# A hybrid decoder step on one core: the head in another order on five engines, past keys and values turned one bank at a time, pooled low halves set between gated products

## The reference, cut to what matters

```python
def compress_kv(kv, w_cmp):               # past rows of the samples: 2048 each
    ch = kv.reshape(B, n_ch, CMP_STRIDE, 2, KV_HEADS, HEAD_DIM)      # CMP_STRIDE = 16
    kc = (einsum('bnjchd,jchd->bnchd', ch[:, :-1], w_cmp[:CMP_STRIDE])
          + einsum('bnjchd,jchd->bnchd', ch[:, 1:], w_cmp[CMP_STRIDE:]))

h = einsum('btd,de->bte', x, w_in)        # layer 0, 3352 columns: values, gates, q, k/v
u = a_val * sigmoid(a_glu)                # then conv, layer norm, attention, w_out

v, gate = split(einsum('btd,de->bte', x, w_in), 2, axis=-1)          # layer 1
d = mean_of_window(v) - v                 # windows 2, 4, 8, 16 on four channel groups
mixed = einsum('btgc,gce->btge', d, w_grp) * scale
y = einsum('bte,ed->btd', mixed * silu(gate), w_out)
```

## Time and profile before

| | |
|---|---|
| median of three runs | 1197.67 us |
| profiled execution, device time | 1204.59 us |
| its span | 1202.9 us |
| PE busy | 1138.5 us (95%) |
| DVE / ACT / POOL busy | 734.9 / 394.8 / 330.4 us |
| chain that ended last, PE's share | 83% |
| DMA moved | 103.17 MB |

### The profile page before, as it was taken

How to read it: one execution, slowest core, us unless ns; L and a number is a source line. 1 busy time by engine, 2 the same in 40 slices (tenths; PEclk the granted TensorE clock), 3 DMA queues, 4 the chain that set the end, 5 groups by cost and what they waited for, 6 DMA issues and landing times.

```text
span 1202.9 us, 17825 instructions
## 1 busy us (share of the span) xinstructions
PE 1138.5 (95%) x7124; PEld 934.8 (78%) x7124; DVE 734.9 (61%) x1360; ACT 394.8 (33%) x838; POOL 330.4 (27%) x340
## 2 busy tenths in 40 slices
PE   5888999999999998999999999899999999989997
PEld 4877999999988854465565655688799999988884
DVE  3467889999883579646544455465555650247645
ACT  3111112122223556565756556411021211244000
POOL 3444530000003577444433434310002212306000
PEclk9899999999999979999999999899999999999999
DMA  6545321353210130004040310832131110131321
GB/s 216 176 158 174 124 89 35 71 196 109 50 40 1 46 140 2 1 1 176 1 176 1 120 57 1 247 120 88 57 92 53 35 52 22 37 140 70 114 96 44
DMA packets 78011, 103.17 MB, mean 86 GB/s; under 512 B 21248, under 2 KB 64392, under 8 KB 76831
## 3 DMA queue, kind: packets, MB, share of 16 engines
q1 hardware_dynamic: 69839, 67.52, 18.2%
q0 software_dynamic: 6016, 33.56, 7.4%
q10 hardware_dynamic: 2080, 1.05, 0.3%
HBM read 90.42 MB, written 16.64 MB: 89 GB/s over the span
## 4 chain that ended last, share of the span: by engine, by line
PE 83%; DVE 8%; DMA 4%; ACT 3%; POOL 1%; issue 1%; SPq 0%; ACTq 0%; POOLq 0%; DVEq 0%
PE PS L681 25%; PE PS L1629 17%; PE PS L1791 14%; PE PS L1165 5%; PE PS L1056 5%; PE PS L1179 4%; PE PS L673 3%; DMA RING<-in_cache_kv_sel,idx 2%; PE PS L1140 2%; PE PS L1094 2%; DVE ACC L548 2%; PE PS L1099 2%; DVE PS L1252 1%; PE PS L1771 1%; DMA idx<-in_page_table 1%
## 5 line engine op out<-in xcount | busy, mean ns | idle before, releaser
L681 PE MATMUL PS<-XH,WH 128*128 128x352 f32 (+1 forms) x648 | 149.2, 335 | 3.1 <-DVE XL L523 3.1
L595 DVE SCALAR_TENSOR_TENSOR Y<-U,SM,Y 128x1024 f32<-128x1024 f32 x120 | 147.4, 1293 | 0.3
L681 PE MATMUL PS<-XL,WH 128*128 128x352 f32 (+1 forms) x648 | 143.7, 326 | 0.0
L681 PE MATMUL PS<-XH,WL 128*128 128x352 f32 (+1 forms) x648 | 143.7, 326 | 0.0
L681 PEld LDWEIGHTS PS<-XH,WH 128*128 128x128 f32 (+1 forms) x648 | 109.0, 188 | 6.5 <-DVE XL L523 3.8
L681 PEld LDWEIGHTS PS<-XL,WH 128*128 128x128 f32 (+1 forms) x648 | 110.5, 188 | 1.4
L681 PEld LDWEIGHTS PS<-XH,WL 128*128 128x128 f32 (+1 forms) x648 | 110.4, 187 | 1.4
L548 DVE SCALAR_TENSOR_TENSOR ACC<-PS,SM,ACC 128x508 f32<-128x508 f32 x124 | 84.0, 740 | 30.7 <-PE PS L673 30.7
L1898 POOL TENSOR_TENSOR WL<-WRAW,WH 128x1024 fp32r<-128x1024 f32 x14 | 37.4, 2673 | 219.8 <-ACT WH L1843 219.8
L1629 PE MATMUL PS<-WOH,XH 128*128 128x512 f32 (+1 forms) x288 | 92.3, 402 | 3.6 <-POOL WOL L1597 3.1
L290 POOL TENSOR_TENSOR WL<-WRAW,WH 128x1024 fp32r<-128x1024 f32 x12 | 28.6, 2385 | 243.2 <-ACT WH L362 235.6
(11 more groups left out here) (316 smaller groups left out, 2057.5 us busy)
## 6 DMA issues: line engine op xcount, KB each, us to landing
WRAW<-in_w_in_even SPq DMA_DIRECT2D x16, 512.0 KB
WRAW<-in_w_in_odd SPq DMA_DIRECT2D x16, 512.0 KB, 4.0
XIN<-in_x_prompt SPq DMA_DIRECT2D x8, 512.0 KB, 12.7
WRAW<-in_w_in_even SPq DMA_DIRECT2D x16, 256.0 KB
TM<-in_state_win_kv SPq DMA_DIRECT2D x8, 512.0 KB, 4.7
XR<-in_x_prompt SPq DMA_DIRECT2D x8, 512.0 KB, 3.5
layer_out<-R SPq DMA_DIRECT2D x8, 512.0 KB, 2.6
XR<-layer_out SPq DMA_DIRECT2D x8, 512.0 KB, 3.2
```

The lines of the kernel that those rows point to most:

```text
L595: v.scalar_tensor_tensor(dst, src, CWT[:, i, t:t + 1], dst, ALU.mult, ALU.add).then_inc(s_cv, 1)
L681: ins = pe.matmul(PS[0:mcols, 3 * slot + c, 0:CH], w[:, slot, kk, 0:mcols], x[:, kk, c * CH:(c + 1) * CH], start=(kk == 0 and n == 0), sto ...
```

## The change

All arithmetic stays. Three places are rewritten.

In the head, ACT's queue loads weight block 0, then the small constants that SP loaded before; weight block 1 is issued after the second tile's XH, and the weights' high halves come one tile later. SP starts with the tiles. POOL makes the identity before the page table's loads, and subtracts WL of block 0 before it waits for the indices. DVE makes six tiles' XL, then the indices, then the other three, then copies the constants. PE turns five tiles first, and the others stand between halves of the column chunks.

In blocks 1 to 8 a pair is turned in two halves, keys and values, at separate steps (24 steps of three matmuls in a block). Each half waits only for its own bank, and DVE's four instructions go in the order: keys of pair p, values of pair p-1, keys of p, values of p.

In the mixer DVE's order is written out anew.

```diff
         def act_program(act):
             load_w(act, 0)
-            load_w(act, 1)
+            act.dma_start(ROWS[0:CW, :], conv_w[0]).then_inc(s_rows, 16)
...
-                if tt == 0:
+                if tt == 1:
+                    load_w(act, 1)
                     high(0)
-                if tt == 5:
+                if tt == 6:
                     high(1)
...
+            low(po, 0)
             po.wait_ge(s_idx, 1)
-            low(po, 0)
             po.wait_ge(s_xt, 12)
             gather(0)
...
+            for tt in range(6):
+                low_x(tt)
             v.wait_ge(s_pt, 16 * 8)
...
+                for q, x, w in ((p, 0, 0), (p - 1, 1, 1), (p, 0, 1), (p, 1, 0)):
+                    if 0 <= q < NPAIR:
+                        compress_half(q, x, w)
...
-            def compress(p):
-                load, group, j = p // 4, p // 16, p % 4
+            def compress(p, x):
+
+                load, j = p // 4, p % 4
                 if p == 0:
                     pe.wait_ge(s_stcu, 1)
                 else:
-                    pe.wait_ge(s_cp, 4 * p)
+                    pe.wait_ge(s_cp, cp_after[(p - 1, x, 1)])
...
+            for tt in range(5):
+                turn_x(tt)
+            first(0, range(4))
+            turn_x(5)
+            first(0, range(4, KT))
+            turn_x(6)
+            turn_x(7)
+            turn_small()
+            first(1, range(4))
+            turn_x(8)
+            first(1, range(4, KT))
...
+                halves = [(h * 3 * KT // (2 * pairs), sum(PAIRS[:m]) + h // 2, h % 2) for h in range(2 * pairs)]
...
+            low_pooled(2)
+            gated(0)
+            low_pooled(3)
+            gated(1)
+            low_pooled(4)
+            low_pooled(5)
+            gated(2)
+            low_pooled(6)
+            gated(3)
+            low_pooled(7)
+            low_gated(0)
+            low_gated(1)
+            for ct in range(4, KT, 2):
+                gated(ct)
+                gated(ct + 1)
+                low_gated(ct - 2)
+                low_gated(ct - 1)
+            low_gated(KT - 2)
+            low_gated(KT - 1)
```

More of the change, by code:

```diff
@@ L54 @@
 LOW_DVE = (10, 25)
+CP_STEPS = [x for p in range(NPAIR + 1) for x in ((p, 0, 0), (p - 1, 1, 1), (p, 0, 1), (p, 1, 0)) if 0 <= x[0] < NPAIR]
+cp_after = {x: n + 1 for n, x in enumerate(CP_STEPS)}
 def width(m):
@@ L299, in link @@
                 po.wait_ge(s_pool, k[0])
-            for r in range(8):
-                po.dma_start(idx[r::8, 0:8], page_table.rearrange("b n -> n b")).then_inc(s_pt, 16)
             link(po.memset(ident[:, :], 0.0))
@@ L305, in pool_program @@
                              pattern=[[-1, P]], channel_multiplier=1).then_inc(s_const, 1)
+            for r in range(8):
+                po.dma_start(idx[r::8, 0:8], page_table.rearrange("b n -> n b")).then_inc(s_pt, 16)
             link(po.iota(idx[:, 48:49], pattern=[[0, 1]], base=0, channel_multiplier=1))
@@ L504, in dve_program, with low_x @@
             v.memset(ACC[:, :, :, NCS:P], 0.0)
+            def low_x(tt):
+                for hf in range(2):
+                    v.wait_ge(s_xh, 2 * tt + hf + 1)
+                    v.tensor_tensor(XL[:, 4 * hf:4 * hf + 4, tok(tt)],
+                                    PS[:, 3 + 2 * (tt % 2) + hf, :].rearrange("p (k t) -> p k t", k=4)[:, :, 0:ntok(tt)],
+                                    XHf[:, 4 * hf:4 * hf + 4, tok(tt)], ALU.subtract).then_inc(s_xl, 1)
+            for tt in range(6):
+                low_x(tt)
             v.wait_ge(s_pt, 16 * 8)
@@ L667, in compress, with block @@
                 else:
-                    pe.wait_ge(s_cp, 4 * p)
+                    pe.wait_ge(s_cp, cp_after[(p - 1, x, 1)])
                 if j == 0:
                     pe.wait_ge(s_xc[load % 2], 64 * (load // 2 + 1))
-                for x in range(2):
-                    for b in range(4):
-                        ins = pe.transpose(PS[:, 6 + x, b * P:b * P + P],
-                                           XC[:, load % 2, b, 256 * j + P * x:256 * j + P * x + P], ident[:, :])
+                for b in range(4):
+                    ins = pe.transpose(PS[:, 6 + x, b * P:b * P + P],
+                                       XC[:, load % 2, b, 256 * j + P * x:256 * j + P * x + P], ident[:, :])
                 ins.then_inc(s_cpt, 1)
-            def block(m, kk, cs=range(3)):
+            def block(m, kk, cs=range(3), halves=()):
                 slot, mcols = m % 2, width(m)
                 for n, (w, x) in enumerate(((WH, XH), (WH, XL), (WL, XH))):
+                    for step, p, side in halves:
+                        if step == 3 * kk + n:
+                            compress(p, side)
                     for c in cs:
@@ L683, in block, with first @@
                 return ins
[L685 to L697 removed]
+            def first(c, kks):
                 pe.wait_ge(s_xl, 6 * c + 6)
@@ L700, in pe_program @@
                     pe.wait_ge(s_wl, 1)
-                for kk in range(KT):
+                for kk in kks:
                     ins = block(0, kk, (c,))
-            ins.then_inc(s_mm, 1)
+                return ins
+            for tt in range(5):
[9 more added lines that the diff above has]
+            first(1, range(4, KT))
+            pe.wait_ge(s_stc, 16)
+            pe.wait_ge(s_smalle, 1)
+            for a in range(2):
+                if a == 0:
+                    pe.wait_ge(s_xl, 16)
+                for i in range(4):
+                    ins = pe.transpose(PS[:, 6 + a, 120 * i:120 * i + 120], STC[:, a, i * P:i * P + P], ident[0:120, 0:120])
+                ins.then_inc(s_small, 1)
+            first(2, range(KT)).then_inc(s_mm, 1)
+            pe.wait_ge(s_const, 2)
             def mean(c):
@@ L728, in one @@
                 pe.wait_ge(s_ev, m + 1)
+                pairs = PAIRS[m] if m < len(PAIRS) else 0
+                halves = [(h * 3 * KT // (2 * pairs), sum(PAIRS[:m]) + h // 2, h % 2) for h in range(2 * pairs)]
                 for kk in range(KT):
-                    for n in range(PAIRS[m] if m < len(PAIRS) else 0):
-                        if kk == n * KT // PAIRS[m]:
-                            compress(sum(PAIRS[:m]) + n)
                     for k, f, c in between:
@@ L735, in one @@
                             f(c)
-                    ins = block(m, kk)
+                    ins = block(m, kk, halves=halves)
                 ins.then_inc(s_mm, 1)
@@ L1949, in dve_mixer, with low_pooled @@
             v.sem_inc(s_d, KT)
-            for ct in range(2, KT):
+            def low_pooled(ct):
                 v.wait_ge(s_dh, ct - 1)
```

94 lines of the change are left out of this document (38 added, 56 removed).

## The result

| | before | after |
|---|---|---|
| median | 1200.05 us (five runs, 1197.24 to 1202.49) | 1188.95 us (five runs, 1188.18 to 1190.60) |
| ratio of the two, 95% interval | | 0.9897 [0.9872, 0.9921] |
| profiled execution | 1204.59 us | 1188.18 us |
| its span | 1202.9 us | 1186.5 us |

The change is faster by 1.0%, 11.1 us between the medians and 16.4 us between the two profiled executions. Why these differ is the first thing that the experiments explain.

What follows compares the result with a forecast made beforehand. PE was taken to bound the kernel, with waits and a lower clock in the head. Head 9.5, pairs 3.7 and mixer 1.2 us sum to 14.4 off a median of 1197.67, giving 1183.3; range 1174 to 1191 us.

Steps and rivals of the forecast that it cites:

- The two terms: Head: first matmul at about 17 us, then 18.5 us of PE work, 12 matmuls of it at the lower clock.
- a second slow stretch: Head: 1 us added for a second stretch at the lower clock, giving an end at 36.5 us.
- early tiles: Head: tiles first on SP's queue, so the first tile lands at 6 to 8 us instead of 11.23.
- the danger of queues that share: Head, rival: weight block 0, loading beside 4 MB of tiles, lands at about 17 us; median 1186.5 us, chance 0.18.
- one of my signs of being wrong: Head: ACT waiting for WRAW between tiles 2 and 3 would show the forecast wrong.
- the head of 39 to 40 us: Head: its end if weight block 0 lands late, 6 to 7 us less than before instead of 9.5; chance 0.18.
- The rival that the waits go away: Blocks 1 to 8 and mixer: two banks decouple DVE and PE fully, the lock costs half; 1171 us, chance 0.12.
- the bound said 14: Blocks 1 to 8: if the waits vanish, 10.4 us more are won, 14 in all.
- the bad bound: Mixer: if DVE's four last low halves precede WOL 4, `kk` = 5 comes at 1103.4, PE's clock falls; 3 us more.
- The hold that I foretold: Mixer: the projection's `kk` = 5, due at 1099.2, waits for WOL 5 until 1100.6; 1.2 us less than before.
- the bound's 6.2 less 1.2: Mixer: 6.2 us won without the lock between DVE and POOL, 1.2 us forecast with it.
- The step that failed: Whole kernel: 14.4 us taken off the median of 1197.67, giving 1183.3 us.

Runs made afterwards that it cites:

- e12: The kernel before with the head's work in the new order but the loads queued as before: 1196.88 us, ratio 0.9958 to before.
- e1: The kernel before with the change's head part alone, loads and order of work: 1197.18 us, ratio 0.9942 to before.
- e9: The kernel before with the head's loads queued as in the change, all work in the old order: 1215.72 us, ratio 1.0098 to before.
- e5: The changed kernel with the values' half always 4 steps behind the keys' half, instead of 2 or 3: 1179.24 us, ratio 0.9794 to before.
- e11: The changed kernel with the values' half 4 steps behind the keys' and weight block 1 rounded behind the last tile: 1179.71 us, ratio 0.9816 to before.
- e8: The changed kernel with POOL filling layer 1's WOL with zeros instead of subtracting, a test only: 1184.76 us, ratio 0.9842 to before.
- e6: The changed kernel with the values' half always 2 steps behind the keys' half: 1201.86 us, ratio 0.9989 to before.
- e7: The changed kernel with the rounding of weight block 1 put behind the last tile: 1188.21 us, ratio 0.9868 to before.
- e10: The changed kernel with weight block 0 loaded first on SP's queue, ahead of the tiles: 1189.50 us, ratio 0.9894 to before.
- the first four experiments: Three runs of the kernel before with the head's, pairs' or mixer's part alone, and one unchanged: 1197.18, 1197.97, 1199.35 and 1204.56 us.
- e2: The kernel before with the change's pairs part alone, so with the old head: 1197.97 us, ratio 0.9949 to before.

## Why the prediction was right, and where not

**Head: right in size, mostly for another reason.** I gave 36.5 us for the end of block 0, the copy starts at 37.06 and the last matmul is at 36.69. The two terms were a first matmul at 17 (18.39) and 18.5 us from there (18.47), plus 1 for a second slow stretch that never came. The errors cancelled: three slow matmuls for twelve, against the stop for weight block 1, which I had not foreseen. The reason that I put first, early tiles, is worth 0.3 to 0.5 us by e12 against e1 and the change, which is within the spread of the heads; it is PE's, DVE's and POOL's order that gains. I named the danger of queues that share only for weight block 0. It came true there in part, and so did one of my signs of being wrong: ACT waited for WRAW between tiles 2 and 3, for 2.80 us, but not until 17, and the head of 39 to 40 us did not come. It came true for block 1 (landed 19 us after its issue) and, in e9, for the small constants.

**Pairs: right.** Foretold 18.7 us a block (74.63 / 4 = 18.66), 14.26 for blocks 5 to 8 (14.34), a half at 0.456 (e5: (15.98 - 11.52) / 10 = 0.446), waits of 0.7 and 0.25 by the gap (0.71 and 0.28). The rival that the waits go away failed because of the gaps, not for want of DVE's time; e5 is that rival, made true by one number: its blocks 1 to 8 take 14.1 us less than before, where the bound said 14.

**Mixer: right in size, wrong in place.** Foretold 1.2 us less, measured 1.5 between the profiles, and by all profiled runs 128.2 to 128.8 for the new order, 130.2 to 131.7 for the old. I had gated low halves and WOL take turns until `kk` = 5 holds the projection at 1100.6. No `kk` waited. The first two gated low halves went back to back (2.42 us from 1064.06), and only then did WOL get its turn (four in 12.51 us from 1065.32); the third and fourth met WOL instead, the gated products behind them came late, and PE stopped for 3.08 us before the projection. PE's clock fell in that stop, which I had put only into the bad bound, and cost 1.6 us more. The hold that I foretold showed itself once, in e11, where PE waited 0.72 us for a WOL 7.9 us into the projection. The exclusion of the two is real and costs what I thought it would (4.9 us by e8, 5 by the bound's 6.2 less 1.2); on which instruction pays I was wrong.

**The sum, and the median.** Profile against profile I gave 1190.2 us and 1188.18 was measured: 2.0 off. The attention stage (from the last copy of BG to the first WOL) took 352.4 us before and 350.2 after, 2.2 less. It took 351.8 to 352.4 in e5, e6, e7, e8 and e10, whose code there is the change's, so I put the 2.2 down to no edit. In e1, e9 and e12 it took 354.0 to 354.2, which took some 2 us from e1's gain; why is open.

The step that failed is the one to the median: I took 14.4 us off 1197.67 and got 1183.3, and it is 1188.95, 5.7 more. Of these, 2.4 are the starting value. 1197.67 was the median of three executions; with five it was 1200.05, and in the four later jobs 1201.4 to 1203.7. The step also called 6.9 us of the profiled execution an excess, and against those later medians the excess is 1 to 3. The other 3.3 are the gain, 11.1 us for 14.4, but the interval of the ratio allows 9.5 to 15.4 us, so these runs do not show that the gain itself was too large.

The heads argue that it was. The step assumed that what a slower execution loses stays in place, and the change takes a part of just that away: the four profiled old heads ended at 46.16, 45.66, 42.36 and 41.02 us, 43.8 in the mean, against 36.5 to 37.3. A typical execution wins 4 to 9 us in the head, as e1's ratio has it (0.9942 [0.9924, 0.9960], 5 to 9 us), where I had 9.5. That the clock differs from execution to execution is seen in the whole kernel too. In the job of the first four experiments the kernel before took 1197.22 to 1200.33 us in the ten executions with the least time, at mean granted clocks of 0.987 to 0.990, and 1203.72 to 1207.11 us in the thirteen with the most, at 0.980 to 0.986. Only profiled executions show in which stage. The range, 1174 to 1191, held the result.

## What to carry to other kernels

Where two engines hand banks to each other, count from the start of one turn to the release of the next and place the turns that many steps apart; a stop costs the bracket's time plus the drain (here 0.5 shown, 0.7 paid). Move a load behind others only together with whatever waits for it: the same queue order cost 9 us or nothing that stands out by what stood first on PE. Before subtracting a profile's gain from a median, look whether the gain is in something that varies from execution to execution, and whether the median itself rests on more than three. A stop just ahead of a long row of matmuls costs more than its length when the clock falls in it (here 3.08 us and 1.6 more).

## What was not expected of the hardware

- A small load behind one weight block on its queue, beside 4 MB on another queue, took 18.5 us to land (e9: issued by 4.1, there at 22.60). On the queue of the tiles but ahead of them it was there by 8.49 in the execution of before.
- With weight block 0 ahead of the tiles on one queue and the small constants first on the other (e10), the first tile was turned at 11.39 us, not at 4.73: a delay of more than five times what 512 KB take at the best rate of the earlier trace rows. Which of the two delays it is open.
- DVE's gated low half takes 1.2 us alone and 3.4 beside POOL's subtractions in a row (6.75 / 2): each waits for about one WOL. Beside POOL's fills of the same size (e8) it stays at 1.2.
- A stop of 3.08 us ahead of the projection let PE's granted clock fall: it was 0.52 from 1078 to 1081 us, and matmuls took 0.43 us for 0.23. In e8, without that stop, none was slow.
- Code and pauses do not fix at which clock a chunk begins. Behind three or four tiles turned without a pause, matmuls ran at 0.16 us, the 2.4 GHz level, from the second on (e2, e12); behind tiles with pauses of 0.4 to 2.9 us between them they began at 0.29, the 1.2 GHz level (before, after), yet behind pauses of 0.84 to 1.95 at 0.16 (e1). Behind the same wait of 1.73 us the second chunk began at 0.29 in before and at 0.16 in e2.
